# Feed-forward activations: low halves of u and of the block sums 128 bytes off their high halves, modulo 256

## What is computed

```python
def swiglu(x, w_gate, w_up, w_down):
    return (jax.nn.silu(x @ w_gate) * (x @ w_up)) @ w_down

def second_block(x, norm_w, ffn_w_gate, ffn_w_up, ffn_w_down, even_w_in, ...):
    h = x                                   # 512 tokens x 1024
    for layer in range(2):
        nw = norm_w[layer]
        f = swiglu(rmsnorm(h, nw[0]), ffn_w_gate[layer, 0], ffn_w_up[layer, 0], ffn_w_down[layer, 0])
        h = h + 0.5 * rmsnorm(f, nw[1])
        u = rmsnorm(h, nw[2])
        m = even_mixer(u, ...) if layer % 2 == 0 else odd_mixer(u, ...)
        h = h + rmsnorm(m, nw[3])
        f = swiglu(rmsnorm(h, nw[4]), ffn_w_gate[layer, 1], ffn_w_up[layer, 1], ffn_w_down[layer, 1])
        h = h + 0.5 * rmsnorm(f, nw[5])
    return h
```

## The kernel before, in words

| tensor | before: high / low modulo 256 | after: high / low |
|---|---|---|
| u (f0 to f3, both projections) | 224 / 224 | 224 / 96 |
| `sums` | 224 / 224 | 224 / 96 |
| `ring`, `spare` of the networks | 32 / 32 | 32 / 32 |
| even projection's weights | 224 / 224 | 224 / 224 |
| odd projection's weights | 160 / 160 | 160 / 160 |
| first block's activations `h_t` and weights `mix_in_w` | 224 / 224 and 160 / 160 | the same |

## Time and profile before

### The profile page before, as it was taken

One profiled execution on the slowest core, in us unless ns is written; L12 is line 12 of the kernel. 1 busy time (PEld: TensorE's weight loads), 2 busy tenths in 40 slices (PEclk: granted clock), 3 DMA queues, 4 the chain that ended last, 5 costly groups with the idle time before them and its releaser, 6 DMA issues. The chain is left out here.

```text
span 3286.9 us, 49236 instructions
## 1 busy us (share of the span) xinstructions
PE 3000.8 (91%) x20670; PEld 2416.6 (74%) x20670; DVE 1681.4 (51%) x2005; ACT 1230.6 (37%) x1958; POOL 368.2 (11%) x250
## 2 busy tenths in 40 slices
PE   6998688877778999999789999999999999799999
PEld 3995563323327998787677998799988875679997
DVE  3228651111128773435356883488532458458743
ACT  4116420000005552435344553455334448445532
POOL 2991001000020000000010000000000005100000
PEclk8998899999998999998899999999999999899999
DMA  6533179999974333131012333234312220233322
GB/s 234 174 115 154 53 261 423 426 426 426 427 299 132 103 116 103 39 103 30 1 64 79 114 118 113 68 103 127 114 55 90 89 66 2 98 94 103 103 97 77
DMA packets 216111, 478.48 MB, mean 146 GB/s; under 512 B 17788, under 2 KB 163671, under 8 KB 203358
## 3 DMA queue, kind: packets, MB, share of 16 engines
q1 hardware_dynamic: 209114, 458.44, 38.7%
q0 software_dynamic: 6480, 15.69, 1.2%
q10 hardware_dynamic: 308, 1.37, 0.1%
HBM read 456.60 MB, written 26.76 MB: 147 GB/s over the span
## 5 line engine op out<-in xcount | busy, mean ns | idle before, releaser
L453 PE MATMUL psum_banks<-u_high,f_ffn_ring 128*128 128x256 f32 (+1 forms) x1408 | 409.7, 291 | 5.6 <-DVE f_ffn_ring L3348 4.7
L454 PE MATMUL psum_banks<-u_low,f_ffn_ring 128*128 128x256 f32 (+1 forms) x1408 | 408.7, 290 | 0.0
L455 PE MATMUL psum_banks<-u_high,f_ffn_ring 128*128 128x256 f32 (+1 forms) x1408 | 408.4, 290 | 0.0
L2070 PE MATMUL psum_banks<-expert_ring,experts_x_t 128*64 128x512 f32 x1024 | 242.0, 630 | 50.2 <-DMA expert_ring<-in_expert_w_up 26.1
L453 PEld LDWEIGHTS psum_banks<-u_high,f_ffn_ring 128*128 128x128 f32 x1408 | 266.8, 190 | 16.0 <-issue 5.9
L454 PEld LDWEIGHTS psum_banks<-u_low,f_ffn_ring 128*128 128x128 f32 x1408 | 266.9, 190 | 6.0 <-issue 0.2
L455 PEld LDWEIGHTS psum_banks<-u_high,f_ffn_ring 128*128 128x128 f32 x1408 | 265.6, 189 | 5.9
L453 PE MATMUL psum_banks<-f_ffn_sums,f_ffn_ring 128*128 128x256 f32 x960 | 267.6, 279 | 1.6 <-issue 1.6
L454 PE MATMUL psum_banks<-f_ffn_sums,f_ffn_ring 128*128 128x256 f32 x960 | 267.4, 279 | 0.0
L455 PE MATMUL psum_banks<-f_ffn_sums,f_ffn_ring 128*128 128x256 f32 x960 | 267.4, 279 | 0.0
L3364 DVE TENSOR_TENSOR f_ffn_ring<-f_ffn_more,f_ffn_ring 128x2048 fp32r<-128x2048 f32 x44 | 100.9, 2292 | 292.7 <-ACT f_ffn_ring L3258 292.7
(11 more groups left out here) (738 smaller groups left out, 7242.2 us busy)
## 6 DMA issues: line engine op xcount, KB each, us to landing
expert_ring<-in_expert_w_gate SPq DMA_DIRECT2D x32, 2048.0 KB, 34.7
expert_ring<-in_expert_w_up SPq DMA_DIRECT2D x30, 2048.0 KB, 35.1
expert_ring<-in_expert_w_down SPq DMA_DIRECT2D x28, 2048.0 KB, 36.6
f_ffn_more<-in_ffn_w_down SPq DMA_DIRECT2D x88, 512.0 KB, 4.4
weight_pieces<-in_ffn_w_gate SPq DMA_DIRECT2D x48, 512.0 KB, 4.6
weight_pieces<-in_ffn_w_up SPq DMA_DIRECT2D x48, 512.0 KB, 6.7
f_ffn_more<-in_ffn_w_gate SPq DMA_DIRECT2D x40, 512.0 KB, 5.1
f_ffn_more<-in_ffn_w_up SPq DMA_DIRECT2D x40, 512.0 KB, 6.9
```

The lines of the kernel that those rows point to most:

```text
L453: nc.tensor.matmul(out, lhs.high, rhs.high, start=start, stop=False, skip_group_check=True)
L454: nc.tensor.matmul(out, lhs.high, rhs.low, start=False, stop=False, skip_group_check=True)
L455: return nc.tensor.matmul(out, lhs.low, rhs.high, start=False, stop=stop, skip_group_check=True)
L2070: last = nc.tensor.matmul(k.ps[half, bank, :], self.xt[:, q, half], self.rows_of(n, a, q * HID, HID), start=q == 0, stop=q == KD - 1)
```

## The change

High and low halves of u come from one tensor instead of two: the low half starts at 128 bytes into it, the high half at 128 bytes behind the end of the low one. A row of `sums` gets 32 elements more (128 bytes) than it uses, so that its low half starts 4224 bytes behind the high half instead of 4096. `made` gets the same shape, and its users cut the 1024 columns out of each row; `first` keeps its two halves as a dimension of their own. No instruction is added, taken out or moved on any engine or queue, none changes its shape, and the addresses of all tensors named in the table above are as it says. The programs' orders differ in line numbers and names alone (`u_high` and `u_low` become one name, `u_split`).

```diff
--- before.py
+++ after.py
@@ -2996,14 +2996,16 @@
 
         if i in (self.T1, self.T2, self.T3):
             at = (self.T1, self.T2, self.T3).index(i)
-            both = self.sums[:, at].rearrange("p c (q n) -> p c q n", q=self.KH)
+            both = self.sums[:, at, :, 0:SUM_COLS].rearrange("p c (q n) -> p c q n", q=self.KH)
             return Split(both[:, 0, q, :], both[:, 1, q, :])
         row = q + (self.KH if i in (self.B21, self.T4) else 0)
         at = self.HALF if i in (self.T4, self.B22) else 0
         return self.u[:, row, at:at + self.HALF]
 
 
-SUMS_SHAPE = [P, 3, 2, Halves.KH * Halves.HALF]
+APART = 32
+SUM_COLS = Halves.KH * Halves.HALF
+SUMS_SHAPE = [P, 3, 2, SUM_COLS + APART]
 
 
 def ffn_products(k, name, raw, u, w_gate, w_up, w_down, hidden, gain, next_gain, ahead, late, out):
@@ -3046,7 +3048,7 @@
         pieces = [raw[:].rearrange("p j n -> p (j n)"), more[:]]
         halves = Halves(u, sums, ring, mixed[:, 0, :], pieces)
         whole = mixed[:, 1, :].rearrange("p (s c n) -> p s c n", s=2, c=2)
-        own = [made[:, i, j, :] for i in range(2) for j in range(2)]
+        own = [made[:, i, j, 0:SUM_COLS] for i in range(2) for j in range(2)]
         post, junk, following, part = own
         seam = Seam(k, s, lambda t: flat(k.ps[:, 2 * t:2 * t + 2, :]), tile_mm, RES, post, following,
                     None if next_gain is None else u, junk, part, raw[:, 1].rearrange("p (j n) -> p j n", j=2), stats[:])
@@ -3079,7 +3081,7 @@
         def sum_split(i):
 
             if i < 3:
-                return Split(*(sums[:, i, j].rearrange("p (q n) -> p q n", q=H.KH) for j in range(2)))
+                return Split(*(sums[:, i, j, 0:SUM_COLS].rearrange("p (q n) -> p q n", q=H.KH) for j in range(2)))
             return u[:, 0:H.KH, H.HALF:]
 
         def hidden_pair(b):
@@ -3379,23 +3381,23 @@
                                         ALU.subtract).then_inc(first_low if n < FIRST - 1 else w_low, 1)
             v.wait_ge(w_high, 2)
             nc.vector.tensor_tensor(classic(1).low, raw[:, 1], classic(1).high.bitcast(F32), ALU.subtract).then_inc(w_low, 1)
-            first = made[:, 2].rearrange("p c (q n) -> p (c q) n", n=H.HALF)
+            first = made[:, 2, :, 0:SUM_COLS].rearrange("p c (q n) -> p c q n", n=H.HALF)
             for kh in range(2):
                 rows = slice(kh * H.KH, (kh + 1) * H.KH)
-                nc.vector.tensor_tensor(first[:, rows, :], u.high[:, rows, 0:H.HALF].bitcast(F32), u.low[:, rows, 0:H.HALF].bitcast(F32),
+                nc.vector.tensor_tensor(first[:, kh], u.high[:, rows, 0:H.HALF].bitcast(F32), u.low[:, rows, 0:H.HALF].bitcast(F32),
                                         ALU.add).then_inc(first_ok, 1)
             v.wait_ge(first_ok, 1)
             for t in (2, 3):
-                nc.vector.tensor_tensor(sum_tile(2, t), first[:, 0:H.KH, (t - 2) * P:(t - 1) * P], seam.banks(t)[:, 0:H.KH, :],
+                nc.vector.tensor_tensor(sum_tile(2, t), first[:, 0, :, (t - 2) * P:(t - 1) * P], seam.banks(t)[:, 0:H.KH, :],
                                         ALU.subtract).then_inc(sum_ok, 1)
             for t in (2, 3):
                 v.wait_ge(sum_ok, t - 1)
                 nc.vector.tensor_tensor(sum_tile(1, t), seam.banks(t)[:, H.KH:, :], sum_tile(2, t), ALU.subtract).then_inc(sum_ok, 1)
             v.wait_ge(first_ok, 2)
             v.wait_ge(sum_ok, 4)
-            nc.vector.tensor_tensor(sum_whole(0), sum_whole(1), first[:, 0:H.KH, :].rearrange("p q n -> p (q n)"),
+            nc.vector.tensor_tensor(sum_whole(0), sum_whole(1), first[:, 0].rearrange("p q n -> p (q n)"),
                                     ALU.add).then_inc(sum_ok, 1)
-            nc.vector.tensor_tensor(sum_whole(3), first[:, H.KH:, :].rearrange("p q n -> p (q n)"), sum_whole(1),
+            nc.vector.tensor_tensor(sum_whole(3), first[:, 1].rearrange("p q n -> p (q n)"), sum_whole(1),
                                     ALU.subtract).then_inc(sum_ok, 1)
             sum_part(0)
             sum_part(1)
@@ -3575,7 +3577,9 @@
 def open_u(k, name):
 
     st = ExitStack()
-    return split_sb(st, k.nc, name, [P, KD, SEQ], side="right"), st
+    whole = st.enter_context(k.nc.sbuf_tensor(f"{name}_split", [P, 2 * (KD * SEQ + APART)], F32R, side="right"))
+    low, high = whole[:, APART:APART + KD * SEQ], whole[:, 2 * APART + KD * SEQ:]
+    return Split(*(x.rearrange("p (q n) -> p q n", q=KD) for x in (high, low))), st
 
 
 def ffn_weights(k, layer, which):
```

## The result

| | before | after |
|---|---|---|
| median of 20 runs each | 3293.3 us | 3299.9 us |
| their spread | 3272.9 to 3304.3 us | 3294.6 to 3308.3 us |
| ratio after / before | | 1.0026, 95% from 1.0015 to 1.0038 |
| the profiled execution's own time | 3288.8 us | 3300.0 us |
| its span | 3286.9 us | 3298.2 us |

(One run of the kernel before, at 5049.2 us, was disturbed and is left out of its spread; without it the median is 3293.1.) The kernel became slower by 0.26%. The forecast was 3273.6 us. The three runs known beforehand had a median of 3287.2; with more of them it is 3293.3. The kernel before spreads over 31 us, the changed one over 14, and what the change took away is the lower part of that spread.

The account below looks back on a forecast made before the run. The prediction took a full PE as the bound, with only matmul pace able to move; -15.1 - 0.6 - 0.4 + 0.9 = -15.2 us from the profiled 3288.8 gave 3273.6 us. Its 8-in-10 range was 3268 to 3304 us.

Parts of the forecast that it names:

- What bounds the kernel: PE is full in the slots, so only matmul pace can move; two steady paces there, 117.8 and 113.3 ns.
- Slots of f0 and f3: 3360 256-wide slot matmuls in these two networks go from 117.8 to 113.3 ns: -15.1 us.
- Slots of f1 and f2: Slot matmuls of these two networks, already at 113.3 ns, stay there: 0, bounds 0 to +15.1 us.
- the slower rival: Alternating distance gives the slots of f1 and f2 the slow 117.8 ns: +15.1 us, 3303.9 us; chance 17%.
- Small terms: Terms outside the slots: classic tiles -0.6, even projection 0 and -0.4, odd projection +0.9 and 0 us.
- Classic tiles: One in three of 384 512-wide matmuls goes to distance 64, from 233.3 to 228.7 ns: -0.6 us.
- Even projection: 512-wide matmuls stay at the floor: 0, bound +3.8 us; a third of the 256-wide changes distance: -0.4 us.
- Odd projection: 192 of 576 512-wide matmuls go from distance 64 to 192: +0.9 us; 256-wide stay at the floor: 0.
- Building the sums and the seams: Building u and sums, the seams and loads, between the networks: same shapes and counts, starts moved by 128 bytes only: 0.
- A matter of chance and stays one: In the slots each network still picks one of two paces: 3288.8 us with two slow, 3273.7 to 3303.9; chance 20%.
- Addresses do not matter: By the skill's rule on weight loads, the 6720 slot matmuls would not move: 3288.8 us; chance 8%.
- The floor goes: Slots drop to 106.7 ns if halves at the same place caused the 6.25%: 44 us more, some 3229 us; chance 5%.

Follow-up runs that it names:

- e1: Kernel before with only u's low half 128 bytes off as in the change, block sums as before: 3295.3 us, ratio 1.0008.
- e2: Kernel before with only the block sums' low half 128 bytes off as in the change, u as before: 3298.2 us, ratio 1.0018.
- e7: Kernel before with u, sums and weights' ring 32 bytes lower, slot operands at multiples of 64 bytes, distance still 192: 3298.5 us, ratio 1.0023.
- e11: Kernel before with an unused matmul of 2 columns ahead of pairs 2 to 10 of each network: 3307.1 us, ratio 1.0034.
- e9: Kernel before with the low halves of the weights' ring entries (stationary) 128 bytes off, distances 192, 192, 64: 3275.0 us, ratio 0.9925.
- e6: Kernel before with the weights' ring 96 bytes higher, uniform slot distance 96: 3316.2 us, ratio 1.0061.
- e13: The same kernel as e9, profiled and timed again: 3276.7 us, ratio 0.9944 against the kernel before.
- e14: e13 with the low half of the first block's stationary operand h_t also moved by 128 bytes: 3274.0 us, ratio 0.9932 against the kernel before.
- e8: Changed kernel with the weights' ring 192 bytes higher, slot distances 0, 128, 0: 3300.2 us, ratio 1.0020 against the kernel before.
- e16: Kernel before with the weights' low half 128 bytes off and the ring moved by 128 bytes, distances 64, 64, 192: 3300.8 us, ratio 1.0018.

## Why the prediction was wrong

**What bounds the kernel** was right: no view but the count in a full window changed, and it explains the time. The reading of two paces and of a phase that persists was right too (e1, e2, e7, e11), with the limit that it persists only from one interruption of the stream to the next.

**Slots of f0 and f3, -15.1 us: the step that failed.** "If the turn of 128 bytes twice in each product keeps the slower phase from holding" — it kept the faster one from holding. Measured: 0 us, x852 twice. The prediction called this "a choice between two observed paces", and that is where it went wrong: each row at 113.3 or 117.8 came from a product with one distance throughout, so none was a row for a product with two. The argument that a phase "that must hold through three unlike matmuls has less to hold on to" picks no direction; it gives no reason why the pace that survives should be the good one. e1 and e2 show 117.8 in just the slots that have the turn, in networks whose other slots run at 113.3. That the turn leaves one pace and not two was right; which one it leaves was a guess.

**Slots of f1 and f2, 0 us.** Measured +13.8, near the upper bound that was given, +15.1. This is the slower rival as written: place f1 and f2, pace 117.8, count 851. Its time, 3303.9, was off by what lies outside: 3300.0 in the profiled execution. Its reason was that the load of the next weights meets the moving stream once in each product; e9 speaks against that, for it has the same meetings and is fast.

**Small terms.** Classic tiles -0.6, measured -0.8. Even projection 0 and -0.4, measured +2.1 and -0.2: distance 128 among its three costs half of the bound of +3.8. Odd projection +0.9 for the 512-wide part, measured +0.9, and its 256-wide part stayed at the floor as forecast, 113.4. Together +2.0 instead of -0.1. Building the sums and the seams: no cost was looked for by itself.

**The other rivals.** "A matter of chance and stays one" holds for the kernel before as far as its pace differs where nothing in the program does, and e7, where other networks are slow, shows it better than any row of before could. It doesn't hold for the change, which is slow in all four of its profiled networks and spreads less: with one network at 113.3 it would be at 3299.9 - 7.6 = 3292.3, and none of its 20 runs is below 3294.6. "Addresses do not matter" fell with e6. That was the prediction's own step from the page it names, which speaks of ports and bandwidth and not of addresses. "The floor goes" fell: 113.3 is the lowest pace of a 256-wide product in every one of the traces.

**The sum against the median.** The spans differ by 11.3 us, the medians by 6.6. The profiled execution of the kernel before had two slow networks; counted from 3273.7 with none, at 7.6 us each, its median of 3293.3 would be 2.6 of them. That fits, but was not counted in profiles, and stays an argument, the more so as a network can change its pace at a break. The forecast used the profiled 3288.8 as its base and so took a lucky draw for the typical one: a change that holds the fast pace is worth more against the median (0.6 to 0.75%, e9, e13, e14) than the forecast's 0.41%, and one that fixes the slow pace costs less.

The predicted 3273.6 us was the right price for four fast networks: e9, e13 and e14 take 3275.0, 3276.7 and 3274.0. Only it is the other operand's offset that gives them.

## What to carry to other kernels

Where TensorE is full and its clock granted, compare counts in equal windows of equal shape; if they differ between stretches with the same program text, operand placement may be a cost to be tuned, and the kernel may have two steady paces, so that one profile or three runs are only a few draws. Treat each layout as unknown until it has been run: of those tried here, one (the low stationary half 128 bytes off at a distance of 192) was 0.6 to 0.75% faster and one 0.9% slower than the kernel before, and no rule drawn from their distances foretold which. A forecast that rests on "it will fall into the better of two observed states" has no row behind it, and its chance should not be above that of the other state.

## What was not expected of the hardware

- The pace of a 256-wide pair of load and matmul in fp32r goes from 113.3 to 120.9 ns by the start addresses of its operands modulo 256 and by the phase, with PE and its loads busy for 100 of 100 us and the clock at 1.00 (2.4 GHz) in each of the windows shown. The Trainium skill, "TensorE: Matmul & The Clock Gate", Part 2, step 1, has two independent read ports and no bandwidth taken by the load. The trace agrees on the overlap; of the ports themselves it shows nothing, but the pace does depend on where both operands lie.
- The phase persists while the stream isn't interrupted: all 1680 slot matmuls of f0 in the kernel before, and through slots that themselves run at another pace (e1, e2). It is lost to one matmul of 2 columns (e11), and can change at a break in the stream, in either direction (117.8 to 113.3 and back in e11, 113.3 to 117.8 in f1 of e7). Two of the distances tried have two paces, and so have two offset layouts (e8, e16).
- The same offset has opposite signs on the two operands: at a distance of 192, moving low half 117.8 in four networks of four, stationary low half 113.4 in twelve of twelve (e9, e13, e14), both 120.9. If uniform networks were fast 5 times in 8, as in the profiles of before and e7, and independent of each other, which e1, e2 and e11 put in doubt, twelve in a row would come by chance 4 times in 1000; the 17 times that all lie below 34 of the kernel before do not rest on that.
- What happens physically is open. No view shows the reads of the two operands, and the runs tell only which layouts are fast. Also open: why no pace lies below 113.3 and 226.7 ns, in both widths 6.25% above the columns divided by 2.4 GHz; e7 rules out only that the remainder modulo 64 makes it.
